# Moving the gate matmuls and one set of ScalarE copies inside the delta core of a two-layer encoder

## Chip, cores and metric

One Trainium2 chip, one core. The metric is the device time of one execution in microseconds (us); several executions of a kernel are timed and their median is given.

## The reference

A two-layer encoder runs over two sequences of 256 tokens (512 in all), width 1024, in float32. Each layer has a mixer, a mixture of 16 experts with expert-chosen tokens, and a gated projection. Layer 0's mixer is attention, layer 1's is a gated delta rule with 8 heads of 128, run forward and backward over chunks of 64 tokens. The part that matters here is that mixer:

```python
proj = h @ w_in                       # q, k, v, z, b, a
z = proj[..., GDN_QKV_DIM:GDN_QKV_DIM + H * GDN_DV]
...
L = jnp.where(strict, jnp.einsum('bhncd,bhnsd->bhncs', kb, k) * decay, 0.0)
T = lax.linalg.triangular_solve(eye + L, eye, left_side=True, lower=True)
u = T @ vb
w = T @ (kb * jnp.exp(gc)[..., None])
...
o = rmsnorm(o, norm_g) * jax.nn.silu(z.reshape(B, S, H, GDN_DV))
return o.reshape(B, S, H * GDN_DV) @ w_out
```

## The kernel before

Each engine has its own written-out program, and the engines meet only at semaphores. Names such as `t1_done` are counters that one engine raises and others wait for. PSUM banks are handed out in rings, and `claim` waits until the bank's last reader is done.

Layer 1's mixer goes through three parts. First the projections of q, k and v. Then `natural` turns k and v, with the first gate products between. Then comes the delta core, a loop over passes p = 0 to 4. Pass p builds the inverse of the triangular blocks of group p, in levels that double the block size, and at the same time applies group p−1. Groups are p = 0 to 3, each with 4 lanes (direction and sequence) of 4 heads.

The gate product z is cut into 8 products `s_z` of 128 tokens by 512 columns, each of 8 steps over the contraction. `gate_part(i, k0, k1)` (L1345) issues steps k0 to k1 of product i on TensorE. Each step is a 128x512 float32 matmul that the profile shows as two instructions. Products 5, 6 and 7 are spread over pass 0, in groups of steps between the level's work. ScalarE reads each finished product with `gate_in` (L884).

The level's work in a pass, on TensorE: `level_turn(p, v)` (L1413) transposes the block matrix, `level_z(p, v)` (L1404) multiplies it with the blocks in `c_m32`, and `level_d(p, v)` (L1426) forms the correction. Between `level_z` and `level_d` stand `spread_u` on ScalarE (L931), which copies the transposed blocks to `c_ux`, and `turn_z` on VectorE (L2124). After `level_d`, `merge` on VectorE (L2133) puts the correction in and transposes (L2108), which raises `t1_done`. `build_kk` and `build_qk` (L1385, L1376) make products of keys and queries for later. `start_level` (L915, L921) and `level_0` (L2116) set up the next group.

When the levels of a group are done, pass p+1 applies the last two doublings on TensorE: `z5` (L1444), `du5` (L1455), `dt5` (L1465), `z6` (L1479, L1480) and `du6` (L1492, L1493). ScalarE serves these with `end_levels` (L943), four 32-partition copies from `c_t1` to `c_t64` that wait for the last `merge`, with `keep` of z5 (L963), which lets `du5` start, with `spread_inverse` (L952) and with `join64` (L959, L960).

GpSimd multiplies decays and masks. Two of its steps touch this change. After the eighth gate product it clears `flat_xt`, the buffer from which the gate steps read, and then copies the diagonal blocks of group 1 into it (L673). `level_z(1, 1)` and `spread_u(1, 0)` use that buffer:

```python
pool.wait_ge(*s_z.full(8))
pool.memset(flat_xt, 0.0).then_inc(zeroed, 1)
pool.wait_ge(zeroed, 3)
spread_m(1)
```

In layer 1's expert stage the weights stream through 8 slots of 2 MB. The first loads wait for the readers of the core's last products (`s_av.freed(15)`) or for steps behind those, and each later load waits until TensorE has used the slot (`w_used`).

Of the kernel before, what the change touches and what calls it, by code (L numbers as in the profile page):

```python
# [21 lines left out]
KD = D // P  # L22
# [101 lines left out]
def trunk_kernel(nc, x_prompt, x_sample, p_prompt, p_sample, norm_mix_g, norm_ffn_g, norm_ple_g,  # L124
# [4 lines left out]
    with ExitStack() as ctx:  # L129
# [265 lines left out]
        for l in range(2):  # L395
# [3 lines left out]
            prev = lay[0] if l else None  # L399
# [369 lines left out]
        def _(act):  # L769
# [68 lines left out]
            def gdn_act():  # L838
# [41 lines left out]
                def gate_in(i):  # L880

                    f, j = i // 4, i % 4
                    act.wait_ge(*s_z.full(i + 1))
                    act.activation(znat[:, j, 4 * f:4 * f + 4, :], psum[:, apply_banks.bank(s_z, i), :].rearrange("p (h w) -> p h w", h=4),  # L884
                                   ACT.Silu).then_inc(s_z.freed(i)[0], 1)
# [48 lines left out]
                def end_levels(q):  # L934

                    act.wait_ge(t1_done, t1_at(q, LEVELS - 1))
                    if q:
                        act.wait_ge(*core["z6"].full(q))
                    if q == 0:
                        act.wait_ge(zeroed, 2)  # L940
                    for g in range(4):
                        gs, u0 = slice(32 * g, 32 * g + 32), 8 * (g // 2)
                        ins = act.activation(c_t64[gs, :, 32 * (g % 2):32 * (g % 2) + 32], c_t1[q % 2][gs, u0:u0 + 8, :], ACT.Copy)  # L943
                    ins.then_inc(t64_done, 1)
# [52 lines left out]
                for p in range(QS + 1):  # L997
                    live, prev = p < QS, p - 1
                    m_prev = prev % 2
                    if live:  # L1000
                        spread_u(p, 0)
                    if p:
                        end_levels(prev)
                        keep(apply_banks, "z5", prev, c_z5, 32)
                        spread_inverse(prev)
                    else:
                        gate_in(5)
                    if p:
                        join64(prev)
                        if p == QS:  # L1010
                            act.wait_ge(o_sum, 1)
                            act.activation(fac[:, F_Y, :, 0:4], fac[:, F_Y, :, 0:4], ACT.Sqrt).then_inc(o_sqrt, 1)
                    if live:
                        spread_u(p, 1)
                    if p:
                        keep(apply_banks, "z6", prev, c_z6, 64)
                    else:
                        exp_decay(1, 0)
                        exp_decay(1, 1)
                    if p >= 2 and p % 2 == 0:  # L1020
                        for a in range(4):
                            keep(apply_banks, "st", 4 * (p // 2 - 1) + a, c_s[a // 2][:, 4 * (a % 2):4 * (a % 2) + 4, :], P)
                    if p in (1, 2):
                        exp_decay(p + 1, 0)
                    if live:
                        spread_u(p, 2)
                    if p == 0:
                        exp_decay(1, 2)
                        exp_decay(1, 3)
                    if p == QS - 1:  # L1030
                        square_out(0, 0)
                        square_out(0, 1)
                    if p and m_prev == 0:
                        for a in (0, 1):
                            keep(apply_banks, "vn", 4 * prev + a, c_vn[:, 4 * a:4 * a + 4, :], P)
                    if p in (1, 2):
                        exp_decay(p + 1, 1)
                        exp_decay(p + 1, 2)
                    if p and m_prev == 0:
                        for a in (2, 3):  # L1040
                            keep(apply_banks, "vn", 4 * prev + a, c_vn[:, 4 * a:4 * a + 4, :], P)
                    if p == QS - 1:
                        square_out(0, 2)
                        square_out(0, 3)
                    if p and m_prev == 1:
                        for a in range(4):
                            keep(apply_banks, "vn", 4 * prev + a, c_vn[:, 4 * a:4 * a + 4, :], P)
                    if p in (1, 2):
                        exp_decay(p + 1, 3)
                    if live:  # L1050
                        spread_u(p, 3)
                    if p + 1 < QS:
                        start_level(p + 1)
                    if p == 0:
                        gate_in(6)
                        gate_in(7)

                def turned(k):

# [97 lines left out]
        def _(pe):  # L1157
# [143 lines left out]
            def gdn_pe():  # L1301
# [237 lines left out]
                for p in range(QS + 1):  # L1539
                    live, prev = p < QS, p - 1  # L1540
                    odd = prev % 2
                    build = p in (1, 2)
                    if live:
                        level_turn(p, 0)
                        level_z(p, 1)
                    if p:
                        z5(prev)
                    else:
                        gate_part(5, 0, 5)
                    if live:  # L1550
                        level_d(p, 1)
                    if p:
                        du5(prev)
                        dt5(prev)
                    else:
                        gate_part(5, 5, KD)
                        gate_part(6, 0, 1)
                    if live:
                        level_turn(p, 1)
                        level_z(p, 2)  # L1560
                    if p:
                        z6(prev)
                    else:
                        gate_part(6, 1, 4)
                        build_kk(1, 0)
                    if p >= 2:
                        for a in range(4):
                            if p % 2 == 0:
                                new_state(p - 2, a)
                            else:  # L1570
                                with_state("qs", p - 2, a)
                            if p == QS and a == 1:
                                du6(prev)
                    if live:
                        level_d(p, 2)
                    if 1 <= p < QS:
                        du6(prev)
                    elif p == 0:
                        gate_part(6, 4, 7)
                        build_kk(1, 1)  # L1580
                    if build:
                        build_kk(p + 1, 0)
                    if live:
                        level_turn(p, 2)
                        level_z(p, 3)
                    if p and odd:
                        for a in range(4):
                            with_state("ks", prev, a)
                    elif p:
                        for a in (0, 1):  # L1590
                            new_values(prev, a)
                    else:
                        gate_part(6, 7, KD)
                        gate_part(7, 0, 2)
                        build_kk(1, 2)
                    if build:
                        build_kk(p + 1, 1)
                        build_kk(p + 1, 2)
                    if live:
                        level_d(p, 3)  # L1600
                    if p == QS:
                        for a in range(4):
                            with_state("qs", prev, a)
                    if p:
                        for a in range(4) if odd else (2, 3):
                            new_values(prev, a)
                    else:
                        gate_part(7, 2, 5)
                        build_kk(1, 3)
                    if build:  # L1610
                        build_kk(p + 1, 3)
                    if live:
                        level_turn(p, 3)
                        level_z(p, 4)
                    if p == QS:
                        turn_heads(0)
                    if p:
                        for a in range(4):
                            attend(prev, a)
                    else:  # L1620
                        gate_part(7, 5, KD)
                    if live:
                        build_qk(p, 0)
                        build_qk(p, 1)
                        level_d(p, 4)
                        build_qk(p, 2)
                        build_qk(p, 3)
                def project_heads(i, half):
# [818 lines left out]
```

## Time and profile before

| | |
|---|---|
| median of 3 runs | 1768.04 us (1766.81 to 1768.09) |
| profiled execution | 1768.09 us, span 1766.3 us |
| TensorE busy (matmul) | 1649.0 us, 93% |
| VectorE, ScalarE, GpSimd busy | 510.0, 462.1, 67.6 us |
| mean granted clock of TensorE | 0.987 |
| delta core, first to last pass | about 967 to 1150 us of the span |
| read from memory | 446.87 MB |

A busy TensorE isn't a TensorE at its peak. The question for an edit inside the core is which wait ends last at each step, which the timeline of each engine shows.

### The profile page before, as it was taken

To read this page: it belongs to the slowest core of one execution; us is meant where nothing else is said; L and a number is where in the kernel's file an instruction comes from. 1 tells how busy PE (TensorE), PEld (TensorE's weight loads), DVE (VectorE), ACT (ScalarE), POOL (GpSimd) and SP (SyncE) were. 2 spreads that over 40 slices of the span, in tenths; PEclk is the share of its full clock that TensorE was granted. 3 is DMA by queue.
4 is the path that set the end of the run, shared out by engine and by line. 5 is a ranking of instruction groups with operands and counts; after the bars stand their busy time and mean duration, and the time that the engine had idled before them with its cause. 6 is when DMAs were issued, how large, how long until landed. Compare 5 with 4: busy or idle time off the path is not lost.

```text
span 1766.3 us, 20627 instructions
## 1 busy us (share of the span) xinstructions
PE 1649.0 (93%) x8757; PEld 784.8 (44%) x8757; DVE 510.0 (29%) x986; ACT 462.1 (26%) x1008; POOL 67.6 (4%) x87
## 2 busy tenths in 40 slices
PE   7999899999889979999999999999999998999888
PEld 4464444443233324444445688854444432433233
DVE  3562311121201213255452356633111211112032
ACT  3232211101011105432225576542111010111053
POOL 2000000000000000000004232000000000000000
PEclk9999999999999999999999999999999999999999
DMA  7008379999999994012120000264699999999931
GB/s 251 0 1 333 119 325 428 428 427 427 429 424 427 428 424 178 1 48 94 49 95 1 2 2 2 97 273 179 277 428 429 427 427 428 424 427 427 426 137 48
DMA packets 50907, 450.30 MB, mean 255 GB/s; under 512 B 4932, under 2 KB 7200, under 8 KB 25600
## 3 DMA queue, kind: packets, MB, share of 16 engines
q1 hardware_dynamic: 50288, 448.67, 61.3%
q8 instruction: 70, 1.15, 0.3%
q0 software_dynamic: 288, 0.22, 0.0%
q14 instruction: 22, 0.17, 0.0%
q10 hardware_dynamic: 239, 0.09, 0.0%
HBM read 446.87 MB, written 2.10 MB: 254 GB/s over the span
## 4 chain that ended last, share of the span: by engine, by line
PE 76%; DMA 15%; ACT 5%; DVE 3%; issue 1%; SPq 0%; DVEq 0%; ACTq 0%
PE banks L1743 28%; PE banks L1183 23%; DMA ring<-in_moe_w_up 7%; DMA ring<-in_moe_w_down 5%; PE banks L1376 4%; PE banks L1634 3%; PE banks L1345 3%; PE banks L1722 2%; PE banks L1771 2%; DMA ring<-in_moe_w_gate 2%; PE banks L1799 2%; PE banks L1266 1%; PE banks L1385 1%; PE banks L1404 1%; PE banks L1752 1%
## 5 line engine op out<-in xcount | busy, mean ns | idle before, releaser
L1743 PE MATMUL banks<-ring,misc 128*64 128x512 f32 x2048 | 459.5, 600 | 33.2 <-DMA ring<-in_moe_w_up 19.9
L1743 PEld LDWEIGHTS banks<-ring,misc 128*64 128x64 f32 x2048 | 147.0, 138 | 318.2 <-issue 278.5
L1743 PE MATMUL banks<-ring,hid_t 128*64 128x512 f32 x976 | 217.5, 595 | 15.4 <-DMA ring<-in_moe_w_down 12.7
L1183 PE MATMUL banks<-ring,xt 128*128 128x512 f32 (+1 forms) x448 | 189.8, 585 | 1.1 <-ACT xt L762 0.6
L2383 DVE TENSOR_TENSOR work<-work,banks 128x512 f32<-128x512 f32 x32 | 33.6, 1052 | 477.1 <-PE banks L1743 477.1
L1183 PE MATMUL banks<-xt,ring 128*128 128x512 f32 x384 | 166.7, 594 | 0.0
L1133 ACT ACTIVATE misc<-banks 32x512 f32<-32x512 f32 x64 | 37.6, 587 | 459.1 <-PE banks L1743 458.8
L1743 PEld LDWEIGHTS banks<-ring,hid_t 128*64 128x64 f32 x976 | 68.4, 137 | 154.8 <-issue 137.4
L1183 PEld LDWEIGHTS banks<-ring,xt 128*128 128x128 f32 x448 | 84.8, 190 | 104.0 <-issue 102.9
L1183 PEld LDWEIGHTS banks<-xt,ring 128*128 128x128 f32 x384 | 72.3, 190 | 91.8 <-issue 89.3
L2398 DVE COPY misc<-banks 32x512 f32<-32x512 f32 x64 | 44.2, 691 | 225.3 <-PE banks L1743 224.8
L1120 ACT ACTIVATE work<-banks 128x512 f32<-128x512 f32 x32 | 19.1, 597 | 217.3 <-PE banks L1743 217.3
L2044 DVE SCALAR_TENSOR_TENSOR misc<-misc,conv_w 128x512 f32<-128x512 f32 x96 | 72.2, 752 | 3.4
L1771 PE MATMUL banks<-misc,xt 128*128 128x512 f32 x128 | 62.3, 620 | 5.4 <-ACT misc L1133 3.1
L1722 PE MATMUL banks<-xt,xn 128*128 128x128 f32 x512 | 59.2, 277 | 2.2 <-DVE xt L2338 2.2
L1722 PEld LDWEIGHTS banks<-xt,xn 128*128 128x128 f32 x512 | 57.8, 192 | 7.2 <-issue 4.9
L1345 PE MATMUL banks<-ring,xt 128*128 128x512 f32 x128 | 57.5, 598 | 0.0
L1376 PEld LDWEIGHTS banks<-ring 128*128 128x128 f32 x384 | 48.3, 197 | 14.3 <-issue 9.3
L1376 PE MATMUL banks<-ring 128*128 128x128 f32 x384 | 51.3, 284 | 3.3 <-DVE ring L2099 1.6
L2373 DVE TENSOR_TENSOR h<-h,banks 128x512 f32<-128x512 f32 x64 | 43.6, 686 | 14.1 <-PE banks L1771 14.1
L736 ACT ACTIVATE work<-h 128x512 f32<-128x512 f32 x40 | 24.8, 620 | 76.8 <-DVE h L1998 42.6
L863 ACT ACTIVATE misc<-banks 128x512 f32<-128x512 f32 x24 | 14.2, 596 | 104.8 <-PE banks L1183 103.6
(317 smaller groups left out, 1541.3 us busy)
## 6 DMA issues: line engine op xcount, KB each, us to landing
ring<-in_moe_w_gate SPq DMA_DIRECT2D x64, 2048.0 KB, 22.2
ring<-in_moe_w_up SPq DMA_DIRECT2D x64, 2048.0 KB, 23.9
ring<-in_moe_w_down SPq DMA_DIRECT2D x58, 2048.0 KB, 25.1
ring<-in_gdn_w_in SPq DMA_DIRECT2D x8, 2048.0 KB, 8.6
ring<-in_ple_w_gate SPq DMA_DIRECT2D x4, 2048.0 KB, 21.5
ring<-in_moe_w_down SPq DMA_DIRECT2D x6, 1024.0 KB, 23.2
ring<-in_mla_w_out SPq DMA_DIRECT2D x2, 2048.0 KB, 23.4
misc<-in_moe_w_down SPq DMA_DIRECT2D x2, 2048.0 KB, 20.9
```

The source lines that it names most:

```text
L1133: ins = act.activation(ybuf[32 * i:32 * i + 32, s, 0:HALF], psum[32 * s:32 * s + 32, 5, :], ACT.Copy)
L1183: mm = pe.matmul(psum[:, banks.bank(st, i), 0:cols], lhs(k), rhs(k), start=(k == 0), stop=(k == n - 1))
L1345: mm = pe.matmul(psum[:, apply_banks.bank(s_z, i), :], xt[:, k, j * P:(j + 1) * P], slot(6 + f, KD, HALF)[:, k, :], start=(k == 0), stop=( ...
L1376: mm = pe.matmul(o, lhs(g), rhs(g), start=True, stop=True)
L1634: mm = pe.matmul(psum[:, banks.bank(s_go, i), :], got[:, k, j * P:(j + 1) * P], gw_out[f][:, k, :], start=(k == 0), stop=(k == KD - 1))
L1722: mm = pe.matmul(o, xn[:, NT * s + t, c0:c0 + P], oh[:, NT * s + t, q * P:(q + 1) * P], start=(t == 0), stop=(t == NT - 1))
L1743: mm = pe.matmul(psum[64 * f:64 * f + 64, bank, :], tokens(4 * kh + k), w[k][:, k, f * HALF:(f + 1) * HALF], start=(kh == 0 and k == 0), s ...
L1771: pe.matmul(psum[:, 6 + g % 2, :], sc[:, q, j, :], ybuf[:, j // NT, f * HALF:(f + 1) * HALF], start=True, stop=True).then_inc(moe_sem["sca ...
L1799: mm = pe.matmul(psum[:, b, :], ptt(l)[:, k, j * P:(j + 1) * P], w_proj(l)[:, k, f * HALF:(f + 1) * HALF], start=(k == 0), stop=(k == 1))
L2044: ins = dve.scalar_tensor_tensor(out=a, in0=x, scalar=w, in1=a, op0=ALU.mult, op1=ALU.add)
L2373: dve.tensor_tensor(hv, hv, psum[:, 6 + g % 2, :], ALU.add).then_inc(moe_sem["scat_free"], 1)
L2398: ins = dve.tensor_copy(ybuf[32 * i:32 * i + 32, s, HALF:D], psum[64 + 32 * s:96 + 32 * s, 5, :])
```

## The change

Two edits. On ScalarE, `end_levels` of group p moves from pass p+1, where it stood after `spread_u(p+1, 0)`, to the end of pass p, ahead of that call. On TensorE, the steps of gate products 6 and 7 in pass 0 are dealt out differently: 3, 2, 2, 2, 2 and 4 steps in the six places between the levels, where it was 4, 3, 3, 3, 3 and 3 (product 5's last three steps counted), and the last 4 steps come in a new place after `level_d(0, 4)`.

```diff
 # ScalarE
                     if p:
-                        end_levels(prev)
                         keep(apply_banks, "z5", prev, c_z5, 32)
                         spread_inverse(prev)
...
                     if p == 0:
                         gate_in(6)
                         gate_in(7)
+                    if live:
+                        end_levels(p)
 # TensorE
                         gate_part(5, 5, KD)
-                        gate_part(6, 0, 1)
...
-                        gate_part(6, 1, 4)
+                        gate_part(6, 0, 2)
                         build_kk(1, 0)
...
-                        gate_part(6, 4, 7)
+                        gate_part(6, 2, 4)
                         build_kk(1, 1)
...
-                        gate_part(6, 7, KD)
-                        gate_part(7, 0, 2)
+                        gate_part(6, 4, 6)
                         build_kk(1, 2)
...
-                        gate_part(7, 2, 5)
+                        gate_part(6, 6, KD)
                         build_kk(1, 3)
...
-                        gate_part(7, 5, KD)
+                        gate_part(7, 0, 4)
                     if live:
                         build_qk(p, 0)
                         build_qk(p, 1)
                         level_d(p, 4)
+                        if p == 0:
+                            gate_part(7, 4, KD)
                         build_qk(p, 2)
                         build_qk(p, 3)
```

## Rows read from the trace of the kernel before

**Rows 1.** The page's chain that ended last, by engine.

```profile
PE 76%; DMA 15%; ACT 5%; DVE 3%; issue 1%; SPq 0%; DVEq 0%; ACTq 0%
```

**Rows 2.** Windows: stretch, length, busy time by engine, clock, DMA share, GB/s.

```profile
1300.00:1400.00 100.00, 99.08 (x470) 38.73 (x470) 17.48 (x29) 11.91 (x22) 0.00 (x0) 0.98 1.01 428
```

**Rows 3.** Timeline of TensorE, pass 0 to 1: start, duration, instructions, [idle before].

```profile
1002.59 2.84 PE L1345 MATMUL banks<-ring,xt 128*128 128x512 f32 x6
1005.27 1.95 PE L1376 MATMUL banks<-ring 128*128 128x128 f32 x16
1007.15 1.08 PE L1426 MATMUL banks<-xn,misc 128*32 128x128 f32 x32
1008.16 2.44 PE L1376 MATMUL banks<-ring 128*128 128x128 f32 x16
1010.44 0.60 PE L1413 MATMUL banks<-ident,misc 128*128 128x128 f32 x4
1011.73 1.08 PE L1404 MATMUL banks<-xt,misc 128*32 128x128 f32 x32 [0.69 <-POOL xt L673]
...
1015.86 1.01 PE L1455 MATMUL banks<-misc 32*32 32x32 f32 x58 [1.01 <-ACT misc L963]
...
1021.93 1.08 PE L1426 MATMUL banks<-xt,misc 128*32 128x128 f32 x32
```

**Rows 4.** Timeline of GpSimd at the same place.

```profile
1005.50 3.51 POOL L698 MEMSET xt<- 128x4096 f32 x1 [35.56 <-PE banks L1345]
1009.08 2.60 POOL L673 COPY xt<-ring 32x512 f32<-32x512 f32 x4
```

**Rows 5.** Timeline of ScalarE, start of pass 1, and one row of pass 2.

```profile
1011.08 2.39 ACT L931 ACTIVATE xt<-banks 32x512 f32<-32x512 f32 x4 [1.51 <-PE banks L1413]
1013.50 1.69 ACT L943 ACTIVATE misc<-misc 32x256 f32<-32x256 f32 x4
1015.21 0.60 ACT L963 ACTIVATE misc<-banks 128x512 f32<-128x512 f32 x1
1015.84 2.55 ACT L952 ACTIVATE ring<-misc 32x512 f32<-32x512 f32 x4
...
1019.19 2.39 ACT L931 ACTIVATE xt<-banks 32x512 f32<-32x512 f32 x4
...
1049.23 2.39 ACT L931 ACTIVATE xt<-banks 32x512 f32<-32x512 f32 x4 [5.56 <-PE banks L1413]
```

**Rows 6.** Timeline of TensorE, start of pass 2.

```profile
1050.14 1.11 PE L1444 MATMUL banks<-misc,ring 32*32 32x32 f32 x64
1051.77 1.08 PE L1426 MATMUL banks<-xt,misc 128*32 128x128 f32 x32 [0.52 <-ACT xt L931]
1054.01 1.01 PE L1455 MATMUL banks<-misc 32*32 32x32 f32 x58 [1.16 <-ACT misc L963]
...
1058.54 3.92 PE L1376 MATMUL banks<-misc,ring 128*128 128x128 f32 x32
```

**Rows 7.** Timeline of TensorE, start of pass 3.

```profile
1098.04 1.01 PE L1455 MATMUL banks<-misc 32*32 32x32 f32 x58 [1.17 <-ACT misc L963]
...
1104.05 2.05 PE L1376 MATMUL banks<-work,ring 128*128 128x128 f32 x16
```

**Rows 8.** Timeline of VectorE: the transposition that ends `merge(1, 4)`.

```profile
1048.86 0.71 DVE L2108 STREAM_TRANSPOSE misc<-misc 128x512 f32<-128x512 f32 x1
```

**Rows 9.** Windows of two us: pass 3, and the end of pass 4.

```profile
1098.00:1100.00 2.00, 1.96 (x96) 1.90 (x96) 0.44 (x1) 1.96 (x4) 0.00 (x0) 0.92 0.03 8
1100.00:1102.00 2.00, 2.00 (x26) 1.61 (x28) 1.31 (x4) 1.93 (x5) 0.00 (x0) 0.50 0.00 0
1102.00:1104.00 2.00, 2.00 (x52) 1.57 (x44) 1.09 (x2) 1.73 (x3) 0.00 (x0) 0.73 0.00 0
...
1148.00:1150.00 2.00, 0.04 (x1) 0.00 (x0) 2.00 (x9) 0.00 (x0) 0.00 (x0) 1.00 0.00 0
1150.00:1152.00 2.00, 1.96 (x12) 1.99 (x13) 2.00 (x9) 0.00 (x0) 0.00 (x0) 0.72 0.00 0
```

## The prediction

> **What bounds the kernel now.** I read the page's chain first: three quarters of the span ends on TensorE and 15% on transfers [rows 1]. The view of windows then says what kind of stretch lies behind the change. The expert stage that follows keeps the 16 DMA engines at a share of 1.01 [rows 2], so I ask there only whether a delay would be absorbed. Layer 1's first expert weights are loaded when the delta core's last results have been read, and each later one when TensorE has used up a slot. The DMA stream is therefore tied to the core's end, and what the core loses or gains should pass on one for one.
>
> The change sits inside that core: passes p = 0 to 4, in which TensorE, VectorE, ScalarE and GpSimd each work through a written-out order. So the rest is read from the timeline, engine by engine. On TensorE, pass 0 ends packed: the last three `gate_part` steps start at 1002.59, two `build_qk` at 1005.27, `level_d(0,4)` at 1007.15, two more `build_qk` at 1008.16, and pass 1 opens at 1010.44 [rows 3]. Pass 0 has no idle time left to fill. Pass 1 has two waits near its start: 0.69 us before `level_z(1,1)`, put down to GpSimd's L673, and 1.01 us before `du5(0)`, put down to ScalarE's L963 [rows 3]. GpSimd's side of the first: it clears the `xt` buffer at 1005.50, right as the last gate step ends, and then makes four block copies into it, from 1009.08 to 1011.68 [rows 4]. That chain is already on the path. ScalarE's side of the second is `spread_u(1,0)` at 1011.08, `end_levels(0)` at 1013.50 for 1.69 us, and only then `keep` of z5 at 1015.21 [rows 5]. Passes 2 and 3 repeat the ScalarE wait alone: 0.52 us before `level_d(2,1)` and 1.16 us before `du5(1)` [rows 6], and pass 3 has 1.17 us in the same place [rows 7].
>
> **The gate steps in pass 0.** The edit removes and adds none; the 16 steps of gates 6 and 7 only slide back in the order. Three steps take 1005.27 − 1002.59 = 2.68 us, 0.89 each with their group's start [rows 3]. What moves is the last one. Before, gate 7 is complete ahead of the two `build_qk` and `level_d(0,4)`. After, both stand in front of it: (1007.15 − 1005.27) + (1008.16 − 1007.15) = 1.88 + 1.01 = 2.89 us, plus about 0.1 for one more group (8 groups in place of 7; an estimate from a `x6` row of 2.84 that hands over after 2.68 [rows 3]). Gate 7 completes 3.0 us later, at about 1008.4 in the old trace's time.
>
> Who waits for it? ScalarE's `gate_in(7)`, which has slack, and GpSimd, whose clearing of `xt` waits for the eighth gate product, since the gate steps read `xt`. The clearing takes 3.51 us and the copies follow after 3.58 [rows 4]. So the copies end at 1011.68 + 3.0 = 1014.7, and `level_z(1,1)`, which reads them, goes from 1011.73 to 1014.7. TensorE reaches this point slightly sooner than before: the old `build_qk` pair at 1008.16 took 2.44 us where the pair before took 1.95 [rows 3], because it waited for a bank. That is worth 0.3 us and is lost in the wait. TensorE then stands still from about 1010.6 to 1014.7, 4.1 us in place of 0.69.
>
> The other end of the edit: fewer gate steps between the levels bring `level_turn(0,3)` and `merge(0,4)` forward by about five steps, 4.3 us. Nothing collects it, since pass 1's start on TensorE is set by the sum of the work and then by GpSimd.
>
> **`end_levels` at the end of the pass.** Four 32-partition copies, 1.69 us together [rows 5], are moved ahead of `spread_u(p+1,0)`; the count is unchanged. ScalarE works in program order, so its wait for `merge(p,4)` now holds back `spread_u(p+1,0)`, and behind that `level_d(p+1,1)`.
>
> Pass 1: `merge(0,4)` is early (above), and `end_levels(0)` runs at about 1009.0 to 1010.7, after `gate_in(7)`, inside GpSimd's delay: cost nothing. If that cover were gone it would cost 1.69 − 1.51, ScalarE's old idle time before L931 [rows 5]. Its removal from between `spread_u` and `keep` of z5 gives back the wait at `du5`. Walk: `level_z(1,1)` 1014.7, z5 at 1015.7, z5's result at 1016.9, `keep` to 1017.5; `level_d(1,1)` 1016.8 to 1017.8. ScalarE's `keep` starts at 1016.9 where it started at 1015.21, and from there `spread_inverse`, `join64` and `spread_u(1,1)` follow back to back [rows 5] and end at 1023.3. `level_d(1,2)` starts at 1023.4, in place of 1021.93 [rows 3]: **+1.45 us**. With the full 3.0 us delay and nothing given back it would be +3.0.
>
> Pass 2: VectorE's last transposition of `merge(1,4)` ends at 1048.86 + 0.71 = 1049.57 [rows 8], while `spread_u(2,0)` started at 1049.23 [rows 5]. After: `end_levels(1)` 1049.61 to 1051.30, `spread_u(2,0)` to 1053.71, `level_d(2,1)` at 1053.86 in place of 1051.77 [rows 6]. It lasts 1.01, so `du5(1)` starts at 1054.87, against 1054.01: **+0.86 us**. z5 is kept by 1054.3 and no longer decides. From there TensorE runs without a gap and the delay stays. Pass 3 is the same pattern (du5 at 1098.04 [rows 7]): **+0.86 us**. Pass 4 has no `spread_u`, and its order on ScalarE is the same in effect: 0.
>
> **The clock.** The granted clock falls from full to half (2.4 to 1.2 GHz) for a short stretch after TensorE had been idle or on small matmuls: in pass 3 the windows show 0.92, 0.50 and 0.73 [rows 9], that is (1 − 0.92) / 0.5 × 2 = 0.32 us, 2 us and 1.08 us, 3.4 us together at half rate. After the 2 us idle at 1148 (0.04 us busy) it falls as well, 0.72 in the next window [rows 9]. A 4.1 us standstill should do so in pass 1. The price: from `du5` to the products after z6, pass 3 took 1104.05 − 1098.04 = 6.01 us, pass 2, at the full clock, 1058.54 − 1054.01 = 4.53 [rows 6, 7]: up to 1.48. In pass 1 part of it lies beside ScalarE's copies: the old pass 1 already had such a stretch after `du5`, mostly under ScalarE's chain. The bounds are 0 (all hidden) and 1.5 (all on `level_z` and z5, ahead of `keep`). I take 0.9, because 0.93 is what `level_z` alone loses, and it is nearest to the end of the standstill.
>
> The Trainium skill ("TensorE: Matmul & The Clock Gate", Terms) puts the penalty of throttled time at that time multiplied by one minus K/N, so half of it here. Applied to such a stretch of 3.4 us this gives an estimate of 1.7 us, and the sum would be 4.9 us instead of 4.1; the trace's 1.48 is close to it but lower.
>
> **Sum.** 1.45 + 0.9 + 0.86 + 0.86 = +4.1 us. The profiled execution took 1768.09 us (span 1766.3), 0.05 above the median of 1768.04. So 1768.0 + 4.1 = **1772.1 us**.
>
> **Rivals.**
> (a) *The clock gives back.* In pass 3 the old run paid 1.48 us; where the low stretch falls depends on the work before it, which has shifted. If it misses pass 3's `du5` stretch and is hidden in pass 1, the sum is 1.45 + 0.86 + 0.86 − 1.48 = +1.7; with only the second, +3.2. For it: pass 2 had the same waits and no low stretch. Time 1769.7 to 1771.2, the "no change" case.
> (b) *The clock costs more.* The standstill before `level_d` in passes 2 and 3 is now in one piece, 1053.86 − 1051.2 = 2.6 us. One more low stretch adds 1.48, and a full price in pass 1 0.6: +6.2, 1774.2.
> (c) *Faster: `end_levels` was the bound and GpSimd is not.* If the clearing of `xt` stopped mattering, pass 1 would lose both waits, 0.69 + 1.01, and if `merge(p,4)` came at least 2 us before `spread_u`'s input in passes 2 and 3 too, another 1.16 + 1.17: −4.0, 1764. It decides once gate 7 ends by 1005.4 and `merge` by 1047. Against it: L673 is named as the releaser now [rows 3], and 1049.57 is later than 1049.23 [rows 5, 8]. It needs GpSimd to start 3 us ahead of the gate step that it waits for.
> (d) *The delay is absorbed later,* in waits on the expert weights: 1768. Against it: those loads start only when slots come free behind the same core.
>
> **Chances.** Forecast and its near neighbours (+3.5 to +5) 0.42; (b) 0.16; (a) 0.25; (d) 0.09; (c) 0.08. What a measurement can tell from no change is about 0.2%, 3.5 us. The forecast and (b) make slower 0.58, (a) and (d) same 0.34, (c) 0.08. The range takes in (a) and (b) and most of (d), and leaves (c) out: 1767.6 to 1775.6. The cases on the slower side alone span 1771.2 to 1775.6.
>
> **What would show it.** In the profile after: GpSimd's L698 waits about 3 us longer, until the last gate step, and TensorE's wait for L673 in pass 1 is near 4 us. In passes 2 and 3 the wait before `du5` on ScalarE's L963 is gone, and the one before `level_d` (L1426) on L931 is about 2.6 us instead of 0.5. L943 sits in front of the first L931 of each pass. The prediction is wrong if `level_z(1,1)` starts less than 2 us late against the end of pass 0, if `level_d(2,1)` does not move, or if the stage after the core starts no later.

## The result, and the profile after

The changed kernel takes 1777.86 us (median of 5, 1775.69 to 1778.77) against 1768.04 us for the kernel before (5 runs, 1766.81 to 1769.66): 9.8 us more, ratio 1.0053 with a 95% interval of 1.0041 to 1.0064. The direction was forecast, the size was not: +4.1 us was expected, and 1777.86 lies above the range, which ended at 1775.6.

The profiled execution took 1776.44 us, with a span of 1774.7 us, 8.4 more than before. First its start: the two executions differ before the change begins. One row of the timeline of TensorE, `level_z(0,1)`, of the kernel before, and then the same row of the kernel after:

```profile
968.00 1.08 PE L1404 MATMUL banks<-xn,misc 128*32 128x128 f32 x32
```

```profile
966.59 1.08 PE L1405 MATMUL banks<-xn,misc 128*32 128x128 f32 x32
```

The new execution reaches the core 1.4 us sooner, so shifts inside the core are read against that. The timeline of TensorE after, passes 0 and 1, which answers to [rows 3]:

```profile
1006.86 1.95 PE L1377 MATMUL banks<-ring 128*128 128x128 f32 x16
1008.64 0.60 PE L1414 MATMUL banks<-ident,misc 128*128 128x128 f32 x4
1013.31 1.94 PE L1405 MATMUL banks<-xt,misc 128*32 128x128 f32 x32 [4.07 <-POOL xt L673]
1015.17 1.74 PE L1445 MATMUL banks<-misc,ring 32*32 32x32 f32 x64
1016.84 1.94 PE L1427 MATMUL banks<-xt,misc 128*32 128x128 f32 x32
...
1024.23 1.08 PE L1427 MATMUL banks<-xt,misc 128*32 128x128 f32 x32 [0.68 <-ACT xt L931]
```

TensorE stands still for 4.07 us before `level_z(1,1)`, put down to GpSimd. Then `level_z` takes 1.94 us in place of 1.08 [rows 3], z5 takes 1.74 in place of 1.11 [rows 6, pass 2], and `level_d` 1.94 in place of 1.08. GpSimd and ScalarE in the same place, which answer to [rows 4, 5]:

```profile
1007.08 3.51 POOL L698 MEMSET xt<- 128x4096 f32 x1 [38.55 <-PE banks L1346]
1010.66 2.60 POOL L673 COPY xt<-ring 32x512 f32<-32x512 f32 x4
```

```profile
1007.68 1.70 ACT L943 ACTIVATE misc<-misc 32x256 f32<-32x256 f32 x4
1010.69 2.39 ACT L931 ACTIVATE xt<-banks 32x512 f32<-32x512 f32 x4 [1.31 <-POOL xt L698]
1016.96 0.60 ACT L963 ACTIVATE misc<-banks 128x512 f32<-128x512 f32 x1 [3.89 <-PE banks L1445]
```

The clearing of `xt` waits 38.55 us where it waited 35.56, the 3.0 us forecast. `end_levels` (L943) runs in the hole ahead of `spread_u`. Passes 2 and 3 on TensorE, which answer to [rows 6, 7]:

```profile
1052.43 1.11 PE L1445 MATMUL banks<-misc,ring 32*32 32x32 f32 x64
1056.15 1.28 PE L1427 MATMUL banks<-xt,misc 128*32 128x128 f32 x32 [2.62 <-ACT xt L931]
1057.37 1.58 PE L1456 MATMUL banks<-misc 32*32 32x32 f32 x58
...
1060.37 1.11 PE L1414 MATMUL banks<-ident,misc 128*128 128x128 f32 x4
1061.41 1.94 PE L1405 MATMUL banks<-xt,misc 128*32 128x128 f32 x32
...
1064.55 3.84 PE L1377 MATMUL banks<-misc,ring 128*128 128x128 f32 x32
...
1104.91 1.58 PE L1456 MATMUL banks<-misc 32*32 32x32 f32 x58
...
1112.20 2.05 PE L1377 MATMUL banks<-work,ring 128*128 128x128 f32 x16
```

The wait before `level_d` is 2.62 us as forecast, and `du5` follows it with no wait of its own. But from `du5` to the products after z6 pass 2 now takes 1064.55 − 1057.37 = 7.18 us, against 4.53. The windows say why. The granted clock is the third column from the end, after the engines' busy times, and these answer to [rows 9]:

```profile
1010.00:1012.00 2.00, 0.00 (x0) 0.00 (x0) 0.00 (x0) 1.29 (x3) 1.82 (x4) 1.00 0.00 0
1012.00:1014.00 2.00, 0.69 (x16) 0.65 (x20) 0.00 (x0) 1.06 (x2) 1.86 (x3) 0.63 0.00 0
1014.00:1016.00 2.00, 2.00 (x61) 1.57 (x56) 0.69 (x1) 0.00 (x0) 2.00 (x3) 0.50 0.00 0
1016.00:1018.00 2.00, 2.00 (x66) 1.85 (x62) 0.03 (x1) 1.02 (x2) 2.00 (x2) 0.50 0.03 8
1018.00:1020.00 2.00, 2.00 (x87) 1.60 (x80) 1.12 (x3) 1.97 (x4) 0.36 (x1) 0.66 0.00 0
...
1056.00:1058.00 2.00, 1.84 (x56) 1.50 (x58) 0.52 (x2) 1.93 (x5) 0.00 (x0) 0.73 0.04 8
1058.00:1060.00 2.00, 2.00 (x77) 2.00 (x73) 1.65 (x4) 1.19 (x2) 0.00 (x0) 0.50 0.00 0
1060.00:1062.00 2.00, 2.00 (x25) 1.57 (x26) 1.00 (x3) 1.23 (x3) 0.00 (x0) 0.50 0.03 8
1062.00:1064.00 2.00, 2.00 (x46) 1.55 (x40) 0.58 (x1) 1.87 (x4) 0.00 (x0) 0.57 0.00 0
```

At half clock in pass 1: (0.37 + 0.5 + 0.5 + 0.34) / 0.5 × 2 = 6.8 us. In pass 2: (0.27 + 0.5 + 0.5 + 0.43) / 0.5 × 2 = 6.8 us. In pass 3 the same windows from 1104 to 1112 read 0.67, 0.50, 0.50 and 0.62, again 6.8 us. Before, such a stretch lasted 3.4 us in pass 3 [rows 9], and pass 2 had none. The two starts of each step give the loss by pass, as the growth of the shift between the two timelines:

| stretch | forecast | measured | from |
|---|---|---|---|
| start of the core | 0 | −1.4 | 968.00 → 966.59 |
| pass 1, to `level_d(1,2)` | +2.35 | +3.7 | 1021.93 → 1024.23 |
| pass 2, to the products after z6 | +0.86 | +3.7 | 1058.54 → 1064.55 |
| pass 3, to the products after z6 | +0.86 | +2.1 | 1104.05 → 1112.20 |
| the rest, to the end | 0 | +0.2 | span 1766.3 → 1774.7 |

### The profile page after: what moved, and what is told of

Its sections match the earlier page's. It is cut to its first block, busy times and chain, and to the rows that moved or that the text cites. A ratio compares the mean times of both kernels' runs of the same rounds, so it can differ in the third digit from the quotient of the medians.

```text
span 1774.7 us, 20627 instructions
## 1 busy us (share of the span) xinstructions
PE 1655.7 (93%) x8757; PEld 790.3 (45%) x8757; DVE 510.1 (29%) x986; ACT 461.9 (26%) x1008; POOL 67.6 (4%) x87
## 4 chain that ended last, share of the span: by engine, by line
PE 75%; DMA 13%; ACT 4%; issue 4%; DVE 3%; POOL 1%; SPq 0%; DVEq 0%; ACTq 0%; POOLq 0%
PE banks L1744 29%; PE banks L1184 22%; DMA ring<-in_moe_w_up 7%; DMA ring<-in_moe_w_down 5%; PE banks L1377 3%; PE banks L1635 3%; PE banks L1772 3%; PE banks L1723 2%; PE banks L1800 2%; PE banks L1346 2%; PE banks L1267 1%; PE banks L1427 1%; PE banks L1753 1%; PE banks L1405 1%; PE banks L1166 1%
```

## Experiments

The question was how much of the 9.8 us is waiting, which the two edits do directly, and how much is the clock. All were timed beside the kernel before on the same chip; its median was 1767.38 us beside e1 to e4, 1766.96 beside e5 to e8 and 1766.94 beside e9 to e11. Ratios are to it, with the 95% interval. "Clock" is the mean granted clock of the profiled execution; the kernel before had 0.987, the changed one 0.982.

| run | median us | ratio | clock |
|---|---|---|---|
| e1_act_only | 1774.50 | 1.0035 (1.0022 to 1.0047) | 0.983 |
| e2_gates_only | 1772.41 | 1.0029 (1.0018 to 1.0040) | 0.982 |
| e3_fillers | 1770.23 | 1.0016 (1.0007 to 1.0025) | 0.990 |
| e4_late_end_levels | 1767.77 | 1.0003 (0.9994 to 1.0011) | 0.988 |
| e5_before_fillers | 1763.96 | 0.9981 (0.9973 to 0.9990) | 0.991 |
| e6_half_clear | 1777.34 | 1.0054 (1.0041 to 1.0067) | 0.980 |
| e7_pass1_filler | 1776.78 | 1.0048 (1.0035 to 1.0060) | 0.982 |
| e8_best | 1767.96 | 1.0005 (0.9996 to 1.0014) | 0.989 |
| e9_gates_filled | 1770.88 | 1.0016 (1.0007 to 1.0025) | 0.986 |
| e10_act_filled | 1767.71 | 1.0005 (0.9996 to 1.0014) | 0.990 |
| e11_pass23_fillers | 1773.13 | 1.0032 (1.0020 to 1.0045) | 0.982 |

**Each edit alone.** The kernel before with only the ScalarE edit:

```diff
-                        end_levels(prev)
                         keep(apply_banks, "z5", prev, c_z5, 32)
...
                         gate_in(7)
+                    if live:
+                        end_levels(p)
```

> Only the ScalarE edit: end_levels at the end of the pass, gate steps dealt out as before. Theory A (each edit makes TensorE stand still, and a low-clock stretch of up to 6.8 us follows): passes 2 and 3 as in the changed kernel, 2.6 us standstill before level_d and together +5.9 us; pass 1 without GpSimd's delay but with level_d(1,1) held by ScalarE, +0.5 to +2.5. Sum +6.4 to +8.4 us, about 1775. Theory B (the gate steps are the main cost, and moving end_levels costs only its waits of 0.86 us in each of passes 2 and 3): about +2 us, 1770.

Measured 1774.50, 6.2 us over by the ratio. That is close to theory A's figure (about 1775), at the low end of its +6.4 to +8.4. Its profiled execution loses 1.5 us in pass 1, where `level_d(1,1)` waits 1.85 us for ScalarE, 3.7 in pass 2 and 2.3 in pass 3. Passes 2 and 3 thus lose about as much as in the changed kernel. The second has only the TensorE edit, with `end_levels` back in its old place:

> Only the TensorE edit: gate steps dealt out late, end_levels where it was. Theory A: one standstill of 4.1 us before level_z(1,1) with a low-clock stretch behind it, +3.7 us in pass 1, passes 2 and 3 as before, about 1771.7. Theory B: the gate steps carry most of the loss, +7 to +8 us, about 1775.5. If it were only the wait, with no clock term: +1.5 to +3.0.

Measured 1772.41, 5.1 us over by the ratio: more than theory A's +3.7 and less than B's. Its executions lie far apart, from 1768.54 to 1776.72 us, and the profiled one, 1775.23, is among the slower. That one had a long low stretch in pass 1. Its window, 15 us long, has a mean clock of 0.55, so (1 − 0.55) / 0.5 × 15 = 13.5 us at half rate:

```profile
1010.00:1025.00 15.00, 12.87 (x289) 10.98 (x290) 4.60 (x9) 9.73 (x19) 6.93 (x8) 0.55 0.01 2
```

The same execution is 5.9 us late after pass 1. It had low stretches in passes 2 and 3 too, 3.4 and 6.8 us, behind the short waits of the kernel before (0.53 and 1.16 us in pass 2); theory A had these passes as before.

So each edit alone loses clearly. Together they lose 9.4 us by the ratio, less than the sum of the two (11.3).

**The standstills filled.** The changed kernel, with matmuls whose product is thrown away in the three standstills. They shorten no wait:

```diff
+                def filler(q, n):
+                    apply_banks.claim(pe, core["du5"], q)
+                    for _ in range(n):
+                        pe.matmul(psum[:, apply_banks.bank(core["du5"], q), :], ident[:, :], tri[:, :, :], start=True, stop=True)
...
                         level_turn(p, 0)
+                        if p == 1:
+                            filler(0, 4)
                         level_z(p, 1)
...
+                    if live and p >= 2:
+                        filler(prev, 3)
                     if live:
                         level_d(p, 1)
```

> The changed kernel with matmuls thrown away in the standstills: 4 of identity by triangle (128x512) before level_z(1,1), 3 before level_d(2,1) and 3 before level_d(3,1), in the bank that du5 will take. They add work and shorten no wait. Theory A (idle time is what lowers the clock): the three stretches of 6.8 us at half clock vanish and with them 5.5 to 6.5 us, so about 1771.5 to 1772.5, what the waits alone cost. Rival (the small 32x32 matmuls are slow there for another reason, and the clock would fall anyway): no gain, or up to 1 us slower than the changed kernel, 1777.5 to 1778.5.

Measured 1770.23, ratio 1.0016: 2.8 us over the kernel before, where the changed kernel is 9.4 over by its ratio. More work on TensorE made it 6.5 us faster, and the time is below theory A's 1771.5 to 1772.5. Its windows over the three places have a full clock:

```profile
1010.00:1020.00 10.00, 9.26 (x296) 7.11 (x294) 4.60 (x9) 7.42 (x14) 6.87 (x8) 1.00 0.01 3
1050.00:1060.00 10.00, 9.35 (x211) 6.92 (x212) 3.99 (x9) 9.20 (x17) 0.93 (x1) 1.00 0.01 3
1098.00:1108.00 10.00, 10.00 (x245) 8.94 (x248) 6.88 (x20) 6.84 (x13) 0.00 (x0) 1.00 0.01 3
```

Its timeline of TensorE gives the price of the waits in passes 1 and 2, which before could only be walked through:

```profile
1012.00 1.08 PE L1405 MATMUL banks<-xt,misc 128*32 128x128 f32 x32 [0.63 <-POOL xt L673]
...
1020.69 1.08 PE L1427 MATMUL banks<-xt,misc 128*32 128x128 f32 x32 [0.79 <-ACT xt L931]
...
1053.70 1.01 PE L1456 MATMUL banks<-misc 32*32 32x32 f32 x58
...
1056.26 0.63 PE L1414 MATMUL banks<-ident,misc 128*128 128x128 f32 x4 [0.65 <-issue]
...
1058.91 3.84 PE L1377 MATMUL banks<-misc,ring 128*128 128x128 f32 x32
...
1099.28 1.01 PE L1456 MATMUL banks<-misc 32*32 32x32 f32 x58
...
1103.80 2.05 PE L1377 MATMUL banks<-work,ring 128*128 128x128 f32 x16
...
1134.82 0.37 PE L1466 MATMUL banks<-misc 32*32 32x32 f32 x4 [2.66 <-issue]
```

This execution has `level_z(0,1)` at 965.29, 2.71 us sooner than before. `level_d(1,2)` at 1020.69 is thus 1020.69 + 2.71 − 1021.93 = 1.47 us late: the 1.45 forecast for pass 1. `du5` of pass 2 is 1053.70 + 2.71 − 1054.01 = 2.40 late, so the wait ahead of it adds 0.93, against 0.86 forecast. The products of pass 2 are 3.08 late; most of the further 0.68 is the 0.65 us before `level_turn(2,1)`, which the trace puts down to no engine ("issue"). The changed kernel's own trace has no such stop there.

A larger stop of that kind, 2.66 us, stands in pass 4 (L1466), with 6.9 us of low clock behind it (a mean of 0.77 over the 15 us from 1130). So this run isn't free of low clock, and its 2.8 us are not the waits alone: they hold this stop, and they lack the low stretch that the kernel before had in pass 3.

**Filled in part.** The same, with the fillers of pass 1 only, and then with those of passes 2 and 3 only:

> The changed kernel with the 4 thrown-away matmuls before level_z(1,1) only. Theory A: pass 1 costs 1.5 us instead of 3.7, passes 2 and 3 keep their standstills and low-clock stretches: 1775.5, 2.3 below the changed kernel. Rival (a low-clock stretch in pass 1 is what brings on those in passes 2 and 3): the later ones go as well and it comes near the run with all fillers, 1770 to 1771.

> The changed kernel with fillers in passes 2 and 3 only, the standstill of 4.1 us in pass 1 left open. Theory A: pass 1 costs 3.7 to 6 us (its low-clock stretch can last 6.8 us or longer), passes 2 and 3 about 2.5 together less the old stretch of pass 3: 1772.5 to 1774.5. Rival (each pass's stretch follows from the one before): as the changed kernel, 1777.

With pass 1 alone 1776.78, only 1.1 us below the changed kernel where 2.3 was expected. Its timeline shows pass 2 opening 2.25 us earlier against the start of the core, as expected, but the low stretch of pass 2 was longer, (0.30 + 0.21) / 0.5 × 10 = 10.2 us in the windows of the profiled execution, and gave more than half of it back:

```profile
1050.00:1060.00 10.00, 7.39 (x220) 6.54 (x212) 4.99 (x11) 7.82 (x15) 0.00 (x0) 0.70 0.01 3
1060.00:1070.00 10.00, 10.00 (x163) 8.80 (x161) 1.72 (x4) 5.37 (x10) 4.03 (x4) 0.79 0.01 2
```

With passes 2 and 3 alone 1773.13, inside theory A's 1772.5 to 1774.5. Windows over the three places, in its profiled execution:

```profile
1014.00:1029.00 15.00, 14.00 (x324) 12.01 (x324) 4.60 (x9) 7.64 (x15) 6.52 (x7) 0.54 0.01 2
1052.00:1062.00 10.00, 9.22 (x210) 6.71 (x212) 6.22 (x12) 5.97 (x12) 1.59 (x2) 1.00 0.01 3
1097.00:1107.00 10.00, 9.22 (x218) 6.71 (x220) 6.22 (x12) 6.08 (x12) 1.49 (x2) 1.00 0.01 2
```

The rivals in which one pass's low stretch brings on the next are out in both directions. Passes 2 and 3 keep theirs when pass 1 has none (its clock is 1.00 from 1010 to 1020 in the first of the two runs), and filled they have none although pass 1 keeps its own, of (1 − 0.54) / 0.5 × 15 = 13.8 us.

**Each edit, filled.** The TensorE edit with the 4 fillers before `level_z(1,1)`, and the ScalarE edit with 2 before `level_d(1,1)` and 3 each before `level_d(2,1)` and `level_d(3,1)`:

> Only the TensorE edit, and its standstill before level_z(1,1) filled with 4 thrown-away matmuls. Theory A (the wait itself costs 1.5 us, the rest is the clock): 1.5 us above the kernel before, 1768.5, and 3 to 4 below the same edit unfilled. Rival (the 3 us later gate product costs its full wait): +3 us, 1770.

> Only the ScalarE edit, with 2 thrown-away matmuls before level_d(1,1) and 3 each before level_d(2,1) and level_d(3,1). Theory A: what is left is the later copies, 1.5 us in pass 1, 1.5 in pass 2 and 1.0 in pass 3, less low-clock stretches of the kernel before that go too (1 to 2 us): +2 to +3, 1769 to 1770, and 4 to 5 below the same edit unfilled. Rival (ScalarE's copies are themselves the 7 us): within 1 us of the unfilled run, 1773.5 to 1774.5.

The ScalarE edit goes from 1.0035 to 1.0005: filled, it costs nothing that can be measured, less than the 1769 to 1770 expected. The expectation had already counted that the fillers take the old stretch in pass 3 away. What it had too high is the waits: in the profiled execution pass 1 is late by 0.15 us, not 1.5, and pass 2 by 1.1, not 1.5. This execution also has a stop of 2.50 us in pass 4 that the trace puts down to no engine.

The TensorE edit goes from 1.0029 to 1.0016. That is 2.8 us over, not 1.5. Its profiled execution shows pass 1 late by the 1.5 us expected, and in pass 3 a mean clock of 0.77 over 15 us, a low stretch of (1 − 0.77) / 0.5 × 15 = 6.9 us; that place is unfilled there and had 3.4 us before, and it puts another 1.4 us on top. Pass 4, unfilled too, has 6.9 us where it had 3.4. So 1.5 of the 2.8 is the wait; the rest goes with low clock in unfilled places, in this execution at least.

**Less waiting for GpSimd.** The changed kernel with the clearing shared (`spread_u(1,0)` also waits for the new counter `xt_high`):

```diff
-                pool.memset(flat_xt, 0.0).then_inc(zeroed, 1)
+                pool.memset(flat_xt[:, 0:2048], 0.0).then_inc(zeroed, 1)
...
                         make_at(p, 3)
+                    if p == 0:
+                        dve.wait_ge(*s_z.full(8))
+                        dve.memset(flat_xt[:, 2048:4096], 0.0).then_inc(xt_high, 1)
```

> The changed kernel, where GpSimd clears only the half of xt that level_z needs (c_m32) and VectorE, idle there, clears the half for spread_u. Theory A: level_z(1,1) starts 1.7 us sooner, the standstill is 2.3 us instead of 4.1; pass 1 gives back 1.5 of its waits and up to 2.2 us of clock, 1774 to 1776.3. Rival (ScalarE's chain sets pass 1, not GpSimd): no change against the changed kernel, 1777.5.

Measured 1777.34, no better than the changed kernel. The wait before `level_z(1,1)` was shortened as meant, to 2.36 us, and pass 2 opened 2.7 us sooner against the start of the core. The low stretches of passes 2 and 3 then lasted 10.2 us each in the profiled execution (means of 0.71 and 0.78 over the two times 10 us from 1050, and of 0.60 and 0.89 from 1100), and ate it up. Why they were longer than in the changed kernel is open. The rival (ScalarE's chain sets pass 1) does not explain this, since pass 1 did get shorter; the expectation that the gain would survive was wrong.

**The other order on ScalarE.** The kernel before, with `end_levels` behind `spread_inverse`:

```diff
-                        end_levels(prev)
                         keep(apply_banks, "z5", prev, c_z5, 32)
                         spread_inverse(prev)
+                        end_levels(prev)
```

> The kernel before with end_levels moved the other way on ScalarE: behind keep of z5 and spread_inverse, ahead of join64. Theory A: the waits before du5 go (1.0, 1.16, 1.17 us in passes 1 to 3), passes 2 and 3 gain 1.1 each, pass 1 nothing since join64 waits for the same four copies; the low-clock stretch of pass 3 may go too (1.5). -2.2 to -3.7 us, 1764.3 to 1765.8. Rival (z6 waits for join64 in every pass, so order among the copies is worth nothing): 1768.

Measured 1767.77, ratio 1.0003, the rival's time. In passes 1 and 2 it is also the rival's reason: the wait before `du5` is gone, and z6 waits for `join64` (L960), behind the same four copies. In pass 3 the low stretch did go, as theory A had it, and `z6` starts 1.1 us sooner. Pass 4, which the expectation left out, took that back: before, the four copies ran beside z5 there; now they stand behind it. The waits before z6 in passes 2 and 4 (the latter was 1.44 us before):

```profile
1055.78 0.27 PE L1479 MATMUL banks<-misc,ring 64*64 64x64 f32 x1 [1.12 <-ACT misc L960]
...
1132.24 0.36 PE L1479 MATMUL banks<-misc,ring 64*64 64x64 f32 x1 [3.07 <-ACT misc L960]
```

**A version that beats both.** The kernel before, its own short waits filled:

```diff
                     if p:
+                        filler("du5", prev, 1)
                         du5(prev)
...
+                    if p == QS:
+                        filler("z6", prev, 1)
                     if p:
                         z6(prev)
...
                         for a in range(4):
+                            if a == 3:
+                                core["qk"].wait_read(pe, 15)
+                                for _ in range(2):
+                                    pe.matmul(psum[:, 4, :], ident[:, :], tri[:, :, :], start=True, stop=True)
                             with_state("qs", prev, a)
```

> The kernel before, its short waits filled with thrown-away matmuls: one before du5 in passes 1 to 4, one before z6 and two before the last with_state in pass 4. Theory A (idle time in the core lowers the clock even before): the low-clock stretches at passes 1, 3 and 4 go, 1 to 4 us gained, 1764 to 1766.5. Rival (a clock stretch in the kernel before costs nothing measurable, or the fillers are late by as much as they save): 1767 to 1769.

Measured 1763.96, ratio 0.9981 (0.9973 to 0.9990): 3.4 us below the kernel before by the ratio, 13 below the changed one by the two ratios. The core, as one window of the kernel before and then of this one, has a mean clock of 0.96 and of 1.00:

```profile
1000.00:1160.00 160.00, 147.08 (x2453) 129.63 (x2452) 94.03 (x206) 100.86 (x218) 34.69 (x33) 0.96 0.08 28
```

```profile
1000.00:1160.00 160.00, 152.26 (x2485) 129.46 (x2485) 97.37 (x213) 104.59 (x242) 34.70 (x33) 1.00 0.09 30
```

In the profiled execution the stretch from `du5` to z6 in pass 3 is 1.4 us shorter than in the kernel before, about the 1.48 us that the low clock cost there.

With the shared clearing added:

> The kernel before with the fillers of the first of these runs and the clearing of xt shared between GpSimd and VectorE. Theory A: the wait of 0.69 us before level_z(1,1) goes, but join64 and spread_u(1,1) on ScalarE still set pass 1; 0 to 0.7 us below the first run of this call, 1763.5 to 1766, below both kernels. Rival: 1767 to 1769.

Measured 1767.96, above the 1763.5 to 1766 expected: a miss. VectorE reaches its clearing only after four `make_at`, and `spread_u(1,0)` then waits for it, so TensorE stands still before `level_d(1,1)`:

```profile
1017.02 1.93 PE L1429 MATMUL banks<-xt,misc 128*32 128x128 f32 x32 [4.30 <-ACT xt L934]
```

One standstill of 4.3 us, with low clock behind it (a mean of 0.89 over the 15 us from 1010, so 3.3 us at half rate), cost the whole gain.

## Why the prediction was wrong

**Gate steps.** Right. Gate 7 ends 3.0 us later (the clearing waits 38.55 against 35.56), TensorE waits 4.07 us for L673 where 4.1 was forecast, and with the clock held up the pass loses 1.47 us against 1.45.

**`end_levels`.** Right: it sits in the hole in pass 1, and in passes 2 and 3 `level_d` waits 2.62 us where 2.6 was forecast. With a full clock `du5` of pass 2 is 0.93 us later for it, against 0.86. For pass 1 without GpSimd's delay the prediction named 1.69 − 1.51 = 0.18 us; the filled ScalarE edit lost 0.15 there.

**The clock.** This is the step that failed. The prediction took 0.9 us in pass 1 and 0 in passes 2 and 3, from a bound of 1.5 us per low stretch that it read in pass 3 of the kernel before. It took the length of a stretch as given, 3.4 us, and put nothing more for passes 2 and 3, without a reason, though it forecast a standstill of 2.6 us in each. Measured were 6.8 us at half rate in each of the three passes. The clock's share can be read from the changed kernel's own timeline:

- Pass 1 lost 3.7 us, of which 1.47 is waiting: 2.2 for the clock.
- Pass 2, from `du5` to the products after z6, took 7.18 us against 4.53: 2.65.
- Pass 3, over the same work, took 1112.20 − 1104.91 = 7.29 us. It was 6.01 before, with a stretch of 3.4 us, and 1103.80 − 1099.28 = 4.52 in the run with all fillers, at full clock. The clock cost 2.8 there, 1.3 more than before.

Together that is 6.2 us more than before, where the prediction had 0.9. The fillers, which give back 6.5 us of 9.4, agree in size. Rival (b) had the mechanism, and priced one more stretch where the stretches had also grown. A smaller slip: the prediction took 0.93 us as what `level_z` alone loses; the traces give 1.94 − 1.08 = 0.86.

The Trainium skill ("TensorE: Matmul & The Clock Gate", Terms) counts throttled time times one minus K/N, half of it here. For 6.8 us that is 3.4 us, as an estimate. The 2.65 and 2.8 us of passes 2 and 3 are below it, as 1.48 was below the 1.7 that it gives for 3.4 us. Its estimate in the prediction came out far too low because of the length put in.

**The sum.** Up to z5 of pass 4 the loss is 9.6 us: about 3.4 of waits (1.47, 1.1 and 0.9; the forecast had 3.17) and 6.2 of clock. Passing on to the end was right: the shift at z5 of pass 4 stays within 0.3 us until the end of the program.

**The rivals.** (a), (c) and (d) did not happen. (a) assumed that low stretches might be lost as the order shifted. In the four profiled executions in which TensorE stood still for 2.6 us in passes 2 and 3 and nothing filled it (the changed kernel, e1, e6, e7), all eight of these passes had one, of 6.8 or 10.2 us.

Open: what sets the length of a low stretch. It was 3.4, 6.8, 10.2 or about 13.5 us in profiled executions, for standstills between 1 and 4.3 us, with no order in the standstill's length that these runs show. A standstill of 4.07 us before the same `level_z(1,1)` was followed by 6.8 us in the changed kernel and by 13.5 in the run with the TensorE edit alone; 4.3 us in the last run was followed by 3.3.

## What to carry to other kernels

In this kernel a standstill of TensorE of 2.6 to 4 us in front of small matmuls cost more than the wait it added: count the wait and then the work behind it at half the clock, and do not take the length of the low stretch from the trace of a better kernel. When moving work to fill one gap, look for the engine that waits for that work's end (here GpSimd's clearing of the operand) and for what stands behind the moved wait in the program of the engine that does the work. Where TensorE must wait anyway, a few matmuls thrown away in a free bank can be worth more than a reordering: they gained 3.4 us in a kernel where neither order of the copies gained anything.

## What the runs showed of the hardware that I had not expected

- The half clock stayed on while TensorE was busy with 32x32 and 32-column matmuls: in pass 2 it ran busy for 1.84 to 2.00 us of every 2 us from 1056 to 1064 and was still at 0.50 to 0.57.
- Four 128x512 float32 matmuls kept the clock up: they took 3.60 us of a wait of some 4.2 us, with 0.63 us left idle, and no fall followed in that pass.
- The kernel before already lost some 3.4 us in its core to low clock behind waits of 1.0 to 2.0 us: filling them raised its core's mean clock from 0.96 to 1.00.
